# Block products of a pair of tiles kept in shared PSUM banks, with three joins and four copies per pair

## The reference

```python
def even_layer(x, norm_g, w_in, pool_w, pool_scale, ws, bs, w_out):
    h = rmsnorm_2(x, norm_g)
    z = h @ w_in
    a, g_a, u, v, g_b = jnp.split(z, [...], axis=-1)
    y_a = multiscale_pool(a, pool_w, pool_scale) * jax.nn.silu(g_a)
    y_b = chunk_spatial_gate(u, v, ws, bs) * jax.nn.silu(g_b)
    return x + jnp.concatenate([y_a, y_b], axis=-1) @ w_out

def odd_layer(x, norm_g, w_in, conv_w, w_out):
    h = rmsnorm_2(x, norm_g)
    z = h @ w_in
    qkv, g_c, d_b, d_c, d_x, g_d = jnp.split(z, [...], axis=-1)
    # three dilated groups of 8 heads of 128, softmax over the groups, silu gate
    # a causal convolution of three taps with gates
    return x + jnp.concatenate([y_c, y_d], axis=-1) @ w_out
```

## Time and profile before

| | us |
|---|---|
| runs | 3325.39, 3325.83, 3329.54; median 3325.83 |
| profiled execution, first to last instruction (span) | 3322.8, mean granted clock 0.970 |
| PE busy | 3117.1 (94%) |
| DVE, ACT, POOL busy | 1872.1, 1262.8, 1611.1 |

### The profile page before, as it was taken

The page is one execution under the profiler, slowest core; times in us unless marked ns, Lnnn a source line. Parts: engine busy times, 40 slices in busy tenths (PEclk is TensorE's granted clock), DMA queues, the critical chain, the costliest instruction groups (busy, mean ns, idle before and its releaser), DMA issues. The chain is left out here.

```text
span 3322.8 us, 43242 instructions
## 1 busy us (share of the span) xinstructions
PE 3117.1 (94%) x15972; PEld 2569.3 (77%) x15972; DVE 1872.1 (56%) x2681; ACT 1262.8 (38%) x2142; POOL 1611.1 (48%) x1056
## 2 busy tenths in 40 slices
PE   6978999887799779999999799999999999999999
PEld 4667888765688657788887688888888888888887
DVE  5666623845799585633531756556556555555712
ACT  5256323714477542222300444444344344222311
POOL 2331332043212147867643566556556556688732
PEclk8989999999899889999999899999999999999999
DMA  8230113174699842222431111111111111222331
GB/s 289 54 84 32 44 38 101 38 253 150 244 395 395 294 141 64 79 76 74 133 127 51 53 48 48 55 39 58 45 43 54 48 55 42 80 74 73 118 101 70
DMA packets 312577, 354.00 MB, mean 107 GB/s; under 512 B 28487, under 2 KB 280299, under 8 KB 306100
## 3 DMA queue, kind: packets, MB, share of 16 engines
q1 hardware_dynamic: 301182, 311.36, 27.9%
q0 software_dynamic: 4608, 16.78, 2.0%
q10 hardware_dynamic: 6582, 23.13, 1.8%
HBM read 293.28 MB, written 54.53 MB: 105 GB/s over the span
## 5 line engine op out<-in xcount | busy, mean ns | idle before, releaser
L2695 POOL TENSOR_TENSOR odd_quarter_lo<-odd_w_sums,odd_quarter_hi 128x512 fp32r<-128x512 f32 x224 | 298.6, 1335 | 279.9 <-ACT odd_quarter_hi L2690 278.3
L2730 PE MATMUL first_z<-odd_t_hi,odd_quarter_hi 128*128 128x512 f32 x784 | 327.7, 418 | 18.3 <-DVE odd_t_lo L4184 18.3
L2730 PE MATMUL odd_z<-odd_t_hi,odd_quarter_hi 128*128 128x512 f32 x784 | 326.0, 416 | 0.8 <-POOL odd_quarter_lo L2695 0.8
L2695 POOL TENSOR_TENSOR odd_quarter_lo<-odd_raw,odd_quarter_hi 128x512 fp32r<-128x512 f32 x168 | 229.8, 1368 | 167.2 <-ACT odd_quarter_hi L2690 162.8
L2732 PE MATMUL first_z<-odd_t_hi,odd_quarter_lo 128*128 128x512 f32 x784 | 308.5, 394 | 0.0
L2732 PE MATMUL odd_z<-odd_t_hi,odd_quarter_lo 128*128 128x512 f32 x784 | 307.3, 392 | 0.0
L2731 PE MATMUL first_z<-odd_t_lo,odd_quarter_hi 128*128 128x512 f32 x784 | 307.2, 392 | 0.0
L2731 PE MATMUL odd_z<-odd_t_lo,odd_quarter_hi 128*128 128x512 f32 x784 | 305.9, 390 | 0.0
L2690 ACT CAST odd_quarter_hi<-odd_w_sums 128x512 fp32r<-128x512 f32 x224 | 139.6, 623 | 365.7 <-PE odd_z L2732 178.9
L2746 DVE SCALAR_TENSOR_TENSOR dil_set<-first_z,dil_set 128x512 f32<-128x512 f32 x196 | 170.6, 883 | 143.4 <-PE first_z L2732 138.5
L2746 DVE SCALAR_TENSOR_TENSOR dil_set<-odd_z,dil_set 128x512 f32<-128x512 f32 x196 | 170.7, 884 | 137.0 <-PE odd_z L2732 132.5
(11 more groups left out here) (624 smaller groups left out, 8219.9 us busy)
## 6 DMA issues: line engine op xcount, KB each, us to landing
odd_raw<-in_odd_w_in SPq DMA_DIRECT2D x224, 256.0 KB, 3.4
raw_gate<-in_w_gate SPq DMA_DIRECT2D x16, 2048.0 KB, 16.1
raw_up<-in_w_up SPq DMA_DIRECT2D x16, 2048.0 KB, 15.8
raw_down<-in_w_down SPq DMA_DIRECT2D x16, 2048.0 KB, 15.6
even_raw<-in_even_w_in SPq DMA_DIRECT2D x80, 256.0 KB, 3.4
start_w_mod<-in_w_mod SPq DMA_DIRECT2D x11, 1024.0 KB, 10.8
w_raw<-in_w_in SPq DMA_DIRECT2D x16, 512.0 KB, 3.7
mix_w_early<-in_w_mod SPq DMA_DIRECT2D x8, 1024.0 KB, 11.8
```

Source lines behind the costliest of these rows:

```text
L2695: pool.tensor_tensor(self.w_lo[:, n % self.SLOTS], self.source(m, i), self.w_hi[:, n % self.SLOTS].bitcast(F32), ALU.subtract).then_inc(se ...
L2730: pe.matmul(to, self.w_hi[:, slot, kt], t_hi[:, kt], start=(kt == 0), stop=False)
```

## The change

The seven products of a pair come in the order A11, S1, S2, A12, S3, S4, A22. Products 0, 2, 4 and 6 (A11, S2, S3, A22) are written to one PSUM bank in turn and not cleared in between, products 1 and 5 (S1, S4) to a second one, product 3 (A12) to a third. ACT copies the bank after products 0, 1, 2 and 6 (to C11, C22, C12 and, complete, C21), DVE joins after 3, 4 and 5 (to C11, C22 and C12). Even pairs use banks 0, 1, 2, odd pairs 3, 2, 1. Each product that adds to a bank waits for the reader of what stood in it before. A semaphore `copied` (4 per pair) and one `joined` (3 per pair) take the place of `p1_out` and `evicted`; whoever waited for a whole pair waits for both (`wait_pair`).

```diff
-            SLOTS, BANKS = 4, 4
-            A11, S2, S3, A22, S1, A12, S4 = range(7)
-            FREE = (0, 1, 2, 3, 5, 6, 7)
+            SLOTS = 4
+            A11, S1, S2, A12, S3, S4, A22 = range(7)
+            JOINED = {3: 1, 4: 2, 5: 3}
+            PLACES = {0: (0, 0), 1: (1, 1), 2: (0, 1), 3: (0, 0), 4: (1, 1), 5: (0, 1), 6: (1, 0)}
...
-                        sp.wait_ge(self.split, 7 * (m - 2) + 4)
+                        sp.wait_ge(self.split, 7 * (m - 2) + 7)
...
+            def bank_of(self, m, i):
+                return ((0, 1, 0, 2, 0, 1, 0), (3, 2, 3, 1, 3, 2, 3))[m % 2][i]
+
+            def wait_pair(self, eng, m, copied=True, joined=True):
+                if copied:
+                    eng.wait_ge(self.copied, 4 * m + 4)
+                if joined:
+                    eng.wait_ge(self.joined, 3 * m + 3)
...
                 pe.wait_ge(self.split, n + 1)
-                if n >= self.BANKS:
-                    of, which = (n - self.BANKS) // 7, (n - self.BANKS) % 7
-                    if which == 0:
-                        pe.wait_ge(self.p1_out, of + 1)
-                    else:
-                        pe.wait_ge(self.evicted, 7 * of + self.FREE[which])
-                to = banks[n % self.BANKS]
+                if i == 0 and m >= 2:
+                    pe.wait_ge(self.copied, 4 * (m - 2) + 4)
+                if i == 1 and m:
+                    pe.wait_ge(self.joined, 3 * (m - 1) + 1)
+                if i == 2:
+                    pe.wait_ge(self.copied, 4 * m + 1)
+                if i == 3 and m:
+                    pe.wait_ge(self.joined, 3 * (m - 1) + 3)
+                if i == 4:
+                    pe.wait_ge(self.copied, 4 * m + 3)
+                if i == 6:
+                    pe.wait_ge(self.joined, 3 * m + 2)
+                to, begins = banks[self.bank_of(m, i)], i in (0, 1, 3)
...
-                    pe.matmul(to, self.w_hi[:, slot, kt], t_hi[:, kt], start=(kt == 0), stop=False)
+                    pe.matmul(to, self.w_hi[:, slot, kt], t_hi[:, kt], start=(begins and kt == 0), stop=False, skip_group_check=True)
...
+            def copy(self, act, m, i, banks, to, scale=1.0):
+                t, half = self.PLACES[i]
+                act.wait_ge(self.product, 7 * m + i + 1)
+                act.activation(to[t][half], self.bank(m, i, banks, to), ACT.Copy, scale=scale).then_inc(self.copied, 1)
+
+            def join(self, dve, m, i, banks, to, scale=1.0):
+                t, half = self.PLACES[i]
+                dve.wait_ge(self.product, 7 * m + i + 1)
+                dve.wait_ge(self.copied, 4 * m + self.JOINED[i])
+                dve.scalar_tensor_tensor(out=to[t][half], in0=self.bank(m, i, banks, to), scalar=scale, in1=to[t][half], op0=ALU.mult,
+                                         op1=ALU.add).then_inc(self.joined, 1)
```

```diff
-                            u2(m)
-                            u3(m)
                             if split:
                                 lo_of_y(0)
-                            c21(m)
+                                lo_of_y(1)
+                            join(m, 3)
                             if split:
-                                lo_of_y(1)
                                 lo_of_y(2)
-                            c22_u4(m)
-                            if split:
                                 lo_of_y(3)
-                            c11(m)
+                            join(m, 4)
                             if split:
                                 lo_of_y(4)
-                            c12(m)
+                            join(m, 5)
```

More of the change, by code:

```diff
@@ L2643, in __init__ @@
                 self.product = sem(f"{tag}_product")
-                self.p1_out = sem(f"{tag}_p1_out")
-                self.evicted = sem(f"{tag}_evicted")
+                self.copied = sem(f"{tag}_copied")
+                self.joined = sem(f"{tag}_joined")
             def load(self, sp, m, tiles, parts=(0, 1)):
@@ L2738, in bank @@
             def bank(self, m, i, banks, to):
[L2739 to L2777, removed]
+                return to[2](banks[self.bank_of(m, i)])
+            def copy(self, act, m, i, banks, to, scale=1.0):
+                t, half = self.PLACES[i]
+                act.wait_ge(self.product, 7 * m + i + 1)
+                act.activation(to[t][half], self.bank(m, i, banks, to), ACT.Copy, scale=scale).then_inc(self.copied, 1)
@@ L3166, in _ @@
                         if k < 2:
-                            pe.wait_ge(quarters.evicted, 7 * (PAIRS - 1) + (5, 7)[k])
+                            if k == 0:
+                                pe.wait_ge(quarters.joined, 3 * (PAIRS - 1) + 1)
+                                pe.wait_ge(quarters.copied, 4 * (PAIRS - 1))
+                            else:
+                                quarters.wait_pair(pe, PAIRS - 1)
                         elif n >= 2 and first == 0:
@@ L3262, in _ @@
                         hi(m, 5)
+                        if m == PAIRS - 1:
+                            for c in range(KT):
+                                split_y(c)
+                        copy(m, 6)
                         hi(m, 6)
[L3265 to L3276 removed]
+                    for c in range(KT, KO):
                         split_y(c)
@@ L3503, in _ @@
-                        if last:
                             lo_of_y(3)
-                        c11(m)
+                        join(m, 4)
                         if last:
                             lo_of_y(4)
-                        c12(m)
+                        join(m, 5)
                     for c in range(5, KT):
@@ L4043, in weights_with_probs @@
                             scale_probs(h - 1, 8, 12)
+                        copy(m, 2)
                         hi(m, 2)
@@ L4069, in _ @@
                         exps(h, 5, 6)
+                        copy(m + 1, 6)
                         hi(m + 1, 6)
```

288 lines of the change are left out of this document (131 added, 157 removed).

## The result

Over 20 runs each, the changed kernel takes 3329.11 us (3326.55 to 3334.24), the kernel before 3324.77 us (3323.18 to 3329.54): a ratio of 1.0015, interval [1.0009, 1.0021], or 3 to 7 us more. Its profiled span is 3326.7 us against 3322.8. 3324.9 was forecast, 0.9 us less than the kernel before; measured are some 4.3 us more. The time lies inside the range, which is 14 us wide, but the sign is wrong. Rival 3 had part of the cause, late joins at the ends of the phases; no rival had the clock that fell behind one of them.

A forecast was written before the change was run, and what follows sets the result against it. PE's own pace, 84 matmuls a pair and busy 94% of the span, was taken as the bound. Terms of 0.0 - 0.3 + 0.3 - 0.9 + 0 + 0.0 = -0.9 us gave 3324.9 us, range 3320.0 to 3334.0.

The forecast's parts named there:

- Rival 3: Late joins at even start, even end and tail reach their upper ends: +3.2 us on the forecast, 3328.1; chance 0.08.
- The tail: Odd layer's last pair and after: new join wait taken as 2.0 us, unit 4's wait gone; net 0.0, -0.6 to +1.9.
- The gain at unit 4: Output projection: `last_x` loaded 3.2 us earlier, so PE's whole wait for `last_w_lo`, 2.04 over its pace, goes.
- End of the even layer: Last even pair: join 4 behind low parts of y comes late for product 6; +0.3 us, 0 to +1.
- Start of the even layer: First even pairs: joins 3 and 4 behind the token lows delay product 6; 0.0 us, -0.5 to +0.6.
- Pool pairs: Even layer: mix starts on time, -1.1 us; POOL lows later at pairs 6 and 8, +0.8; net -0.3, -1.7 to +1.5.
- Start of the odd layer: Pair 1: lows end earlier, POOL's second sum runs short, product 0 starts earlier; -0.9 us, -1.2 to +0.2.
- Heads and conv pairs: Middle of the odd layer: PE has no removable wait, copies and joins are covered; cost 0.
- the score loop: Heads: score's bank free at 2150.8, half a microsecond of slack before the next score; cost 0.
- Rival 1: Score loop in heads: slack overrun by 0.7 us in each of 16 pairs, 11.2 us slower, 3336; chance 0.12.
- Rival 4: Scores: each added wait costs PE 51 ns, 192 scores, +9.8 us, 3334.7; chance 0.05.
- joins don't hold POOL up: Pairs: taking 304 joins from DVE frees POOL of nothing; the opposite view would credit 1 us more.

The follow-up runs named there:

- e1: Changed kernel with join 4 ahead of the low parts of y 2 and 3 in the odd layer's last pair; 3329.53 us, ratio 1.0012.
- e4: Changed kernel with join 4 ahead of the low parts of y 2 and 3 in both layers' last pairs; 3326.19 us, ratio 1.0001.
- e2: Kernel before, with the low parts of y 0 to 3 between first and second join of the odd layer's last pair; 3327.53 us, ratio 1.0008.
- e7: Kernel before, with the weights of unit 4 of the odd output projection loaded ahead of `last_x`; 3323.21 us, ratio 0.9993.
- e3: Changed kernel with the low part of y 3 made in two instructions, the join of product 4 between them; 3328.05 us, ratio 1.0008.
- e9: e4 with each copy of ACT made in four instructions of a quarter of the columns; 3327.60 us, ratio 1.0010 to the kernel before.
- e8: e4 with each copy of ACT made in two instructions of half the columns; 3328.94 us, ratio 1.0011 to the kernel before.
- e5: e4 with the weights of unit 4 of the odd output projection loaded ahead of `last_x`; 3323.60 us, ratio 0.9994 to the kernel before.

## Why the prediction was wrong, step by step

**The tail: mis-sized, and a term missing.** This is the step that failed. It was "a new wait of 1.5 to 3.9, of which I take 2.0", less 2.04 at unit 4: net 0.0. Measured is +3.5. The wait was real, at the place and for the cause named, but 3.3 us: I took a value near the lower end because POOL would be less in the way, and POOL was in the way (2.88 and 3.23 us for `last_w_hi` and `last_w_lo` beside it, DVE's low parts at 2.3 to 2.8 each). The 2.77 us that the step takes for one low part come from the earlier trace rows, whose instruction is 128x2048; that a 128x1024 part of y took 2.77 us too, at 3118.75 of the trace of before, saved the bound.

The gain at unit 4, 2.2 us, was right in size by luck. The step had it from a load of `last_x` 3.2 us earlier. Against the kernel before, by the matmul's number, the last low part of y came 0.1 us earlier (3151.60 + 1.22 against the earlier trace rows, less the 0.6 us by which the changed kernel's profile is ahead there), and so did POOL's weights of unit 4:

```profile
3167.70 1.89 POOL L3768 TENSOR_TENSOR last_w_hi<-last_w_raw,zero_col 128x1024 fp32r<-128x1024 f32 x1 [8.61 <-DMA last_w_raw<-in_odd_w_out]
```

The wait went because PE came 5.7 us late, and with PE on time it is back, at 2.8 and 2.4 us (e1, e4). DVE had time for the low parts, but then waited 2.0 us at 3144.28 for a cast, and ACT for a load of y. So the join's wait had no gain of its own to stand against.

What was missing is the clock: no term, bound or rival had it. From 0.8 us before the end of the wait the clock was 0.50 for 6.8 us, 2.5 us lost, which is the whole distance between the upper end that I gave (+1.9) and a tail of +3.5, and more. The trace of before has such a place, around the end of the 6.2 us wait of the earlier trace rows (window; PE busy, clock, DMA share, GB/s):

```profile
1851.90:1858.70 6.80, 3.31 (x8) 0.50 0.00 0
```

**End of the even layer.** +0.3 was taken, "from 0 to +1"; it was +0.99. The mechanism, join 4 behind four low parts, is the one of the tail, and e4 takes both away.

**Start of the even layer.** 0.0, from -0.5 to +0.6, against +0.50: product 6 came 1.6 us late for join 4, and 1.1 of that came back at pair 1, where the weights had been waited for. The step had 0.8 to 2.0 for the first and 1.4 for the second; its place is right, and the value lies near the upper end.

**Pool pairs.** -0.3 was forecast and 0.00 measured, of two terms that were both there: the lateness rises by 1.2 by pair 8 (waits for `even_quarter_lo`, 0.35 and 1.10) and falls by 1.2 at the first mix matmuls, whose wait is gone.

**Start of the odd layer.** -0.9 was forecast, +0.29 measured. POOL, then ACT:

```profile
1863.99 2.62 POOL L2696 TENSOR_TENSOR odd_quarter_lo<-odd_raw,odd_quarter_hi 128x512 fp32r<-128x512 f32 x1 [0.68 <-ACT odd_quarter_hi L2691]
1866.77 3.13 POOL L2704 TENSOR_TENSOR odd_w_sums<-odd_raw 128x512 f32<-128x512 f32 x1 [0.17 <-POOL odd_quarter_lo L2696]
1870.05 1.29 POOL L2707 TENSOR_TENSOR odd_w_sums<-odd_w_sums,odd_raw 128x512 f32<-128x512 f32 x1
...
1872.67 1.28 POOL L2696 TENSOR_TENSOR odd_quarter_lo<-odd_raw,odd_quarter_hi 128x512 fp32r<-128x512 f32 x1
```

```profile
1862.80 0.60 ACT L2763 ACTIVATE dil_set<-first_z 128x512 f32<-128x512 f32 x1 [1.66 <-PE first_z L2751]
1863.29 0.61 ACT L2691 CAST odd_quarter_hi<-odd_raw 128x512 fp32r<-128x512 f32 x1
```

The second sum did run at 1.29 us instead of 3.15, as the step had it. But the chain began 1.3 us later (1866.77, against 1865.44 in the earlier trace rows), 2.2 by the matmul's number, which takes the 1.9 back: the low part ahead of it waits for a cast that now stands behind a copy (1862.80, 1863.29), and took 2.62 us itself. I had moved the end of POOL's chain and not its start. Between executions of kernels that are the same there, this stretch varies by 0.3 (e2 and e7) and more, so what is shown is that the gain of 0.9 didn't come, not that 0.3 was lost.

**Heads and conv pairs.** Right: 0.00 in ten profiles. The covers are there, some thinner than worked out: from the end of a copy to the product that waits for it 1.4 us or more (2.7 for the worst), and from a join 1.68 in heads (1.9 for the worst), 1.83 in conv pairs, and 0.81 in the first pair of the layer. For the score loop the bank was to be free at 2150.8, with half a microsecond to spare, and it is 0.63. The two rows don't belong together, though: two banks take turns, and the bank of the score at 2151.43 was freed by the bias ahead of the one shown, at 2149.92, so that the kernel before had 1.5 us there. The timeline of DVE, then that score in PE's; the first bias waited for ACT and frees the score's bank at 2150.22:

```profile
2149.74 0.48 DVE L4240 SCALAR_TENSOR_TENSOR dil_biased<-const,odd_aux 128x256 f32<-128x256 f32 x1 [2.82 <-ACT dil_p L4007]
...
2150.59 0.34 DVE L4240 SCALAR_TENSOR_TENSOR dil_biased<-const,odd_aux 128x128 f32<-128x128 f32 x1
...
2150.85 0.59 PE L3804 MATMUL odd_aux<-dil_set 128*128 128x256 f32 x2
```

Rival 1 (0.12) is out: the bank frees in time in each head. Rival 4, a price of 51 ns for a wait, is out by the head period of 120.84 us with 24 scores in it. That joins don't hold POOL up fits too: with 304 of 532 gone POOL's busy time is 1610.6 us against 1611.1, and in the head period 70.36 against 70.60. The rule of the Trainium skill that was quoted for it ("SBUF — State Buffer", "Who interferes with whom") agrees.

**Rival 3** (0.08), late joins at the ends, was the true one in its mechanism, with its upper ends reached or nearly (+0.5, +1.0) and passed in the tail; 3328.1 is also the nearest of the forecasts to the measured time. Its reading, that several terms of unknown size all have their bad side in one place (low parts ahead of joins in a last pair), spoke for a higher chance: the upper ends hang together, for the same DVE instructions beside the same POOL work stretch in all of them.

**Open:** what decides whether the clock falls. Of waits of PE in a busy stretch of this layer, 1.9 us (kernel before) and 2.4 (e4) left it up; 2.6 (e3, e9), 2.8 (e1), 3.2 (the change) and 3.25 (e2) had half clock for 3.4 or 6.8 us; another of 2.8 (e8) had not. Where it was 6.8 us (the change, e9) the clock had fallen 0.5 to 0.8 us before PE resumed, where it was 3.4 (e1, e2, e3) 0.2 to 1.0 us after. The same code has the fall in one execution and not in another, as e1 and e4 show at unit 4. The Trainium skill, "TensorE: Matmul & The Clock Gate", section "HAM oscillation — how this bites in real kernels", has it that a wait for data in the middle of a kernel can drop the clock, so that the work behind it begins slow; the traces in which the clock fell agree, and price it here: 1.4 to 2.9 us on top of the wait. The edge of the score loop and whether e5 beats the kernel before are open too.

## What to carry to other kernels

When a kernel is at one engine's pace, taking work from another one brings nothing, and what moves the time is the order in which the moved pieces queue at the places where the phase ends: look there for each consumer (here the last product) that now waits for a producer behind unrelated work. Price a stall of PE like those seen here, 2.6 us and more, with what the clock may take behind it, not with its own length alone. To find 5 us in 3300 whose runs vary by as much, compare two traces by the number of the instruction, stretch by stretch: where PE runs at its own pace an untouched stretch reads 0.00, and each cause shows by itself. Where PE waits for others or the clock changes, compare two executions of the same code first, to see what such a stretch can read from nothing. And when a wait is gone, ask whether what it waited for came earlier or the waiter later.

## What the runs showed of the hardware that was not expected

Half clock behind a wait cost 0.20 us for each matmul (0.43 instead of 0.23) at a granted clock of 0.50: 14 of them in the change, 2.5 us in all. It can fall in one execution and not in another of the same code (unit 4 after waits of 2.8 us in e1 and 2.4 in e4). A copy by ACT from PSUM to a strided target takes as long in four instructions as in one (1.11 and 1.11 us for 128x512), a contiguous one does not (0.79 against 0.60). The first block, unchanged, differs by up to 8 us between two executions, more than the effect measured here.
